# State-space chunks placed between the convolution branch's matmul units of a two-block transformer kernel

## What is computed

```python
h = x @ w_in
sc_b, sc_c, sc_h, z, xbc, dt_raw = _split(h, [...])
y_a = sc_b * causal_dwconv(sc_c * sc_h, sc_conv_w)               # convolution branch, 3 taps
xs, bm, cm = _split(silu(causal_dwconv(xbc, ssm_conv_w, ssm_conv_b)), [...])
# state-space branch: 4 chunks of 128 tokens, 16 heads of 64, 2 groups, state 128
seg = exp(where(causal, a_cs[t] - a_cs[s], -inf))                # a_cs: running sum of dt * a
cb = einsum('bctgn,bcsgn->bcgts', cc, bc)
y_diag = einsum('bcgts,bcgrts,bcsgrp->bctgrp', cb, seg, xdt)
y_off = cc @ (state carried from the chunks before), scaled by exp(a_cs)
y = y_diag + y_off + d_skip * xs
y_b = gated_rmsnorm(y, z, norm_g)
mixer = concatenate([y_a, y_b]) @ w_out
```

## Time and profile before

| | |
|---|---|
| time, median of 3 runs | 2885.03 us |
| time of the profiled execution | 2883.41 us |
| span of its trace | 2881.5 us |
| PE busy in the span | 2821.4 us |
| DVE, ACT, POOL busy | 1341.6, 1078.1, 1147.8 us |
| DMA, mean over the span | 104 GB/s |

### The profile page before, as it was taken

How to read it: one execution, slowest core, us unless ns; L and a number is a source line. 1 busy time by engine, 2 the same in 40 slices (tenths; PEclk the granted TensorE clock), 3 DMA queues, 4 the chain that set the end, 5 groups by cost and what they waited for, 6 DMA issues and landing times.

```text
span 2881.5 us, 37694 instructions
## 1 busy us (share of the span) xinstructions
PE 2821.4 (98%) x13730; PEld 2306.2 (80%) x13730; DVE 1341.6 (47%) x1532; ACT 1078.1 (37%) x1524; POOL 1147.8 (40%) x472
## 2 busy tenths in 40 slices
PE   9998799999999999999989999999999999999999
PEld 8787588888878778888877778888888888888887
DVE  4332837885345457886347753113332742321232
ACT  4322244333344344334344653234342323432332
POOL 4442044444434203444424223444434434444443
PEclk9999799999999999999999999999999999999999
DMA  5332025763233104873323013332343223333332
GB/s 158 93 94 67 0 88 182 242 217 102 81 99 92 52 8 131 259 239 108 102 66 100 2 52 88 95 103 94 102 125 102 83 79 102 95 88 95 105 99 73
DMA packets 319809, 299.90 MB, mean 104 GB/s; under 512 B 16268, under 2 KB 251224, under 8 KB 319576
## 3 DMA queue, kind: packets, MB, share of 16 engines
q1 hardware_dynamic: 304680, 236.70, 27.9%
q10 hardware_dynamic: 15024, 61.75, 6.3%
HBM read 296.30 MB, written 2.11 MB: 104 GB/s over the span
## 4 chain that ended last, share of the span: by engine, by line
PE 45%; issue 37%; POOL 16%; DVE 1%; ACT 0%; POOLq 0%; DVEq 0%; ACTq 0%
POOL wlo L548 16%; PE ps L1992 7%; PE ps L1993 7%; PE ps L1994 7%; PE ps L1850 6%; PE ps L1851 6%; PE ps L1852 6%; PE ps L2222 1%; PE ps L2165 1%; PE ps L2191 1%; PE ps L2297 1%; PE ps L2016 0%; PE ps L2018 0%; PE ps L2017 0%; PE ps L1855 0%
## 5 line engine op out<-in xcount | busy, mean ns | idle before, releaser
L548 POOL TENSOR_TENSOR wlo<-raw,whi 128x1024 fp32r<-128x1024 f32 x444 | 1122.6, 2531 | 1695.3 <-ACT whi L606 1695.0
L1850 PE MATMUL ps<-xhi,whi 128*128 128x512 f32 x1824 | 714.7, 392 | 1.8 <-DVE pb L1233 1.5
L1852 PE MATMUL ps<-xhi,wlo 128*128 128x512 f32 x1824 | 710.1, 389 | 0.0
L1851 PE MATMUL ps<-xlo,whi 128*128 128x512 f32 x1824 | 709.9, 389 | 0.0
L606 ACT ACTIVATE whi<-raw 128x1024 fp32r<-128x1024 f32 x444 | 466.2, 1051 | 343.4 <-PE ps L1994 171.9
L1992 PE MATMUL ps<-whi,ahi 128*128 128x512 f32 x1184 | 463.0, 391 | 8.9 <-issue 7.8
L1994 PE MATMUL ps<-whi,alo 128*128 128x512 f32 x1184 | 462.3, 390 | 0.0
L1993 PE MATMUL ps<-wlo,ahi 128*128 128x512 f32 x1184 | 462.2, 390 | 0.0
L1850 PEld LDWEIGHTS ps<-xhi,whi 128*128 128x128 f32 x1824 | 342.4, 188 | 74.3 <-DVE pb L1233 1.9
L1852 PEld LDWEIGHTS ps<-xhi,wlo 128*128 128x128 f32 x1824 | 342.3, 188 | 71.7
L1851 PEld LDWEIGHTS ps<-xlo,whi 128*128 128x128 f32 x1824 | 342.5, 188 | 69.3
(11 more groups left out here) (277 smaller groups left out, 2940.7 us busy)
## 6 DMA issues: line engine op xcount, KB each, us to landing
adaraw<-in_ada_w ACTq DMA_DIRECT2D x64, 768.0 KB, 6.1
raw<-in_ffn_w_up SPq DMA_DIRECT2D x88, 512.0 KB, 4.0
raw<-in_mlp_w_in SPq DMA_DIRECT2D x64, 512.0 KB, 4.1
raw<-in_mlp_w_out SPq DMA_DIRECT2D x64, 512.0 KB, 3.6
raw<-in_gmlp_w_in SPq DMA_DIRECT2D x48, 512.0 KB, 3.8
raw<-in_sc_ssm_w_in SPq DMA_DIRECT2D x44, 512.0 KB, 3.8
raw<-in_ffn_w_down SPq DMA_DIRECT2D x44, 512.0 KB, 3.6
raw<-in_fox_w_in SPq DMA_DIRECT2D x24, 512.0 KB, 3.8
```

The source lines that it names most:

```text
L548: pool.tensor_tensor(wlo[:, j], raw[:, j], whi[:, j].bitcast(F32), ALU.subtract).then_inc(w_lo, 1)
L1850: pe.matmul(out, lh, rh, start=start, stop=False)
L1851: pe.matmul(out, lh, rl, start=False, stop=False)
L1852: return pe.matmul(out, ll, rh, start=False, stop=stop)
```

## The change

The units of `z` come right after those of `xbc`, and their silu is taken then. The 16 units of `scp` and the 8 of `scb` are written out one by one (`pe_mix`, `act_mix`, `dve_mix`, v = 0 to 23), and behind fixed ones of them each engine does a piece of the state-space work on banks 0 to 3, which the units don't use: the transposes behind units 0 to 2 (`TOK_AT`), the running sums behind 3 (`CUMS_AT`), and for each chunk the decay matrix (`R_AT`), the C B product and the carried part (`CB_AT`), an addition (`OFF_IN_AT`), and the head matmuls with the state (`Y_AT`).

The decay matrix is made in another way. PE transposes the running sum of each head, broadcast over 128 columns, 16 transposes a chunk; ScalarE takes relu(a_s - a_t) per head straight out of PSUM (16 instructions of 128 by 128, with `scale=-1` and the sum as bias), and then exp(-x). `gbuf`, the matmuls with ones, DVE's subtraction and its clamp are gone. y is built up in place in `xs_tok`, and `xdt`, `xdd` have one buffer each. The 32 transposes in front of the second part of `out0` are split in two groups of 16, behind its second and its third unit.

```diff
+UNITS = [("xbc", 12), ("z", 8), ("scp", 16), ("scb", 8), ("out0", 16), ("up0", 44), ("dn0", 22),
          ("fqk", 16), ("fv", 8), ("fo", 8), ("up1", 44), ("dn1", 22), ("qkv", 12), ("o", 8),
          ("mu0", 32), ("md0", 32), ("gv", 24), ("gu", 24), ("go", 24), ("mu1", 32), ("md1", 32)]
...
+MIX = 24
+TOK_AT, CUMS_AT = (0, 1, 2), 3
+R_AT = (4, 9, 14, 19)
+CB_AT = (5, 10, 15, 20)
+OFF_IN_AT = (6, 11, 16, 21)
+Y_AT = (7, 12, 17, 21)
...
+    mbuf = arena("mbuf", [P, 16, P], 32)
+    ssd_sq = arena("ssd_sq", [P, 2, HALF], 32)
+    xdt = arena("xdt", [P, D], 40)
+    xdd = arena("xdd", [P, D], 44)
+    y_off = arena("y_off", [P, D], 76)
+    prev = arena("prev", [P, D], 80)
+    cbm = arena("cbm", [P, 2, P], 84)
...
         sp_f(sp, "xbc", w_in0, XBC_COL)
+        sp_t(sp, "z", w_in0, 4, [ZCOL, ZCOL + HALF])
         sp_pairs(sp, "scp", w_in0, SC_C, SC_H, 16)
         sp_f(sp, "scb", w_in0, SC_B)
-        sp_t(sp, "z", w_in0, 4, [ZCOL, ZCOL + HALF])
...
+        for v in range(MIX):
+            act_whi(act, S + AHEAD, v, v % 4)
+            if v < 16 and v % 2:
+                i, b = v // 4, v % 4 // 2
+                act.wait_ge(unit_done, S + v + 1)
+                if i:
+                    act.wait_ge(sc_step, 8 * i + 4 * b - 6)
+                act.activation(hb[:, b], ps[:, bank_f(v)], ACT.Copy).then_inc(sc_h, 1)
+            act_ssd_at(act, v)
+
...
+            act.wait_ge(dts, 15)
+            act.activation(sm[:, 12], sm[:, 15], ACT.Exp).then_inc(dta, 1)
+            act.activation(sm[:, 13], sm[:, 11], ACT.Exp).then_inc(dta, 1)
+            act.activation(sm[:, 14], ps[:, 0, 64:128].rearrange("p (c h) -> p c h", c=NT), ACT.Exp).then_inc(dta, 1)
...
+        if v in R_AT:
+            c = R_AT.index(v)
+            if c:
+                act.wait_ge(ssd_mm, c)
+                act.wait_ge(gt_sq, 2 * c)
+            for h in range(HEADS):
+                if h % 8 == 0:
+                    act.wait_ge(ssd_r, 2 * c + h // 8 + 1)
+                act.activation(mbuf[:, h], ps[:, h // 4, (h % 4) * P:(h % 4 + 1) * P], ACT.Relu, scale=-1.0,
+                               bias=sm[:, 11, c, h:h + 1]).then_inc(ssd_d, 1)
             for g in range(2):
-                act.wait_ge(ssd_d, 4 * c + 2 * g + 2)
-                act.activation(mbuf[:, 8 * g:8 * g + 8], mbuf[:, 8 * g:8 * g + 8], ACT.Exp).then_inc(ssd_e, 1)
-            if c:
-                act_gate_squares(act, c - 1)
-
-    def act_gate_squares(act, t):
-        act.wait_ge(gt_u, t + 1)
-        for g in range(2):
-            if t or g:
-                act.wait_ge(gt_sq, 2 * t + g)
-            act.activation(ssd_sq[:], y_tok[:, t, g * HALF:(g + 1) * HALF], ACT.Square,
-                           accum_out=sumsq[:, t, g:g + 1]).then_inc(gt_sq, 1)
+                m = mbuf[:, 8 * g:8 * g + 8]
+                act.wait_ge(ssd_d, 16 * c + 8 * g + 8)
+                act.activation(m, m, ACT.Exp, scale=-1.0).then_inc(ssd_e, 1)
+        if v in Y_AT:
+            c = Y_AT.index(v)
+            act.wait_ge(gt_u, c + 1)
+            for g in range(2):
+                act.activation(ssd_sq[:, g], xs_tok[:, c, g * HALF:(g + 1) * HALF], ACT.Square,
+                               accum_out=sumsq[:, c, g:g + 1]).then_inc(gt_sq, 1)
...
-        act.wait_ge(ssd_mm, 4)
+        act.wait_ge(scb_done, 8)
         split(0, 0, 0, 0)
         split(1, 0, 0, 1)
-        act_gate_squares(act, NT - 1)
         act.wait_ge(gt_sq, 8)
         act.activation(mv[:], sumsq[:], ACT.Sqrt, scale=1.0 / HALF, bias=eps_ln[:, 0:1]).then_inc(gt_std, 1)
...
+    def dve_scp(dve, v):
+
+        i, b = v // 4, v % 4 // 2
+        k, s = 2 * i + b, 8 * i + 4 * b + 1
+        y = ya_yb[:, k]
+        dve.wait_ge(sc_h, k + 1)
...
+        for v in range(MIX):
+            if v < 16 and v % 2:
+                dve_scp(dve, v)
+            dve_ssd_at(dve, v)
+            if v >= 16:
+                e = v - 16
+                if e == 0:
+                    dve.wait_ge(sc_step, 33)
+                dve.wait_ge(unit_done, S + v + 1)
+                dve.tensor_tensor(ya_yb[:, e], ps[:, bank_f(e)], ya_yb[:, e], ALU.mult).then_inc(scb_done, 1)
...
+        if v in R_AT:
...
+            dve.tensor_tensor(heads(xdt[:]), x, bc_h(sm[:, 9, c]), ALU.mult).then_inc(ssd_x, 1)
...
-            dve.wait_ge(ssd_x, 2 * c + 1)
...
+            dve.tensor_tensor(heads(xdd[:]), heads(xdt[:]), bc_h(sm[:, 12, c]), ALU.mult).then_inc(ssd_x, 1)
+            dve.tensor_tensor(x, x, bc_h(small[:, 2]), ALU.mult).then_inc(ssd_y, 1)
+        if v in CB_AT:
...
+            dve.wait_ge(ssd_cb, c + 1)
+            dve.tensor_tensor(cbm[:], ps[:, 0, 0:256].rearrange("p (g t) -> p g t", g=2),
+                              tri.unsqueeze(1).to_broadcast([P, 2, P]), ALU.mult).then_inc(ssd_cbm, 1)
+            if c:
+                dve.wait_ge(ssd_off, c)
+                dve.tensor_tensor(heads(y_off[:]), ps[:, 2:4].rearrange("p b (h d) -> p (b h) d", d=HD),
+                                  bc_h(sm[:, 13, c]), ALU.mult).then_inc(ssd_y, 1)
...
-            for g in range(2):
                 dve.wait_ge(ssd_e, 2 * c + g + 1)
...
+                dve.tensor_tensor(m, m, cbm[:, g].unsqueeze(1).to_broadcast([P, 8, P]), ALU.mult).then_inc(ssd_m, 1)
+        if v in OFF_IN_AT[1:]:
+            c = OFF_IN_AT.index(v)
+            dve.wait_ge(ssd_y, 4 * c)
+            dve.tensor_tensor(xs_tok[:, c], xs_tok[:, c], y_off[:], ALU.add).then_inc(ssd_y, 1)
...
+                dve.wait_ge(ssd_prev, 2 * c - 1)
+                dve.tensor_tensor(heads(prev[:]), heads(prev[:]), bc_h(sm[:, 14, c]), ALU.mult).then_inc(ssd_prev, 1)
...
             dve.wait_ge(ssd_mm, c + 1)
             if c < NT - 1:
...
-            ystep(dve.tensor_tensor(y, ps[:, 4:6].rearrange("p b n -> p (b n)"), y, ALU.add))
+            dve.wait_ge(ssd_y, 4 * c + 1)
+            dve.tensor_tensor(y, ps[:, 0:2].rearrange("p b n -> p (b n)"), y, ALU.add).then_inc(ssd_y, 1)
...
             dve.tensor_tensor(y, y, zs[:, c], ALU.mult).then_inc(gt_u, 1)
...
                 unit(1, 0, 0, False)
+                if mid:
+                    mid(pe)
                 unit(2, 0, 0, False)
                 head(pe)
...
+        S = U0["z"]
+        for h in range(2):
+            if h == 0:
+                pe.wait_ge(xbc_conv, 36)
+            else:
+                pe.wait_ge(dts, 1)
...
+        for v in range(MIX):
+            if v >= 20:
+                pe.wait_ge(scb_done, v - 19)
+            elif v >= 4:
+                pe.wait_ge(sc_step, 8 * (v // 4) + 4 * (v % 4 // 2) - 6)
+            pe.wait_ge(w_lo, S + v + 1)
...
+            ins.then_inc(unit_done, 1)
+            pe_ssd_at(pe, v)
...
+        if v in TOK_AT:
+            if v == 0:
+                pe.wait_ge(xbc_silu, 12)
+                pe.wait_ge(z_done, 8)
+            for g in range(4 * v, 4 * v + 4):
...
+        if v in R_AT:
+            c = R_AT.index(v)
+            if c == 0:
+                pe.wait_ge(dts, 15)
+                pe.wait_ge(dta, 6)
+            else:
+                pe.wait_ge(ssd_y, 4 * c - 2)
+                pe.wait_ge(ssd_prev, 2 * c - 1)
+            for h in range(HEADS):
+                ins = pe.transpose(ps[:, h // 4, (h % 4) * P:(h % 4 + 1) * P],
+                                   sm[:, 11, c, h:h + 1].to_broadcast([P, P]), ident)
+                if h % 8 == 7:
+                    ins.then_inc(ssd_r, 1)
...
+            pe.wait_ge(ssd_d, 16 * c + 8)
...
+            ins.then_inc(ssd_cb, 1)
             if c:
-                pe.wait_ge(ssd_y, ny[c - 1])
+                pe.wait_ge(ssd_d, 16 * c + 16)
...
+        if v in Y_AT:
+            c = Y_AT.index(v)
...
             for h in range(HEADS):
                 if h % 8 == 0:
                     pe.wait_ge(ssd_m, 2 * c + h // 8 + 1)
...
+        pe_z(pe)
+        pe_mix(pe)
+        pe_t_jit(pe, "out0", q=1, free=lambda h: ((ssd_y, 14),) if h == 0 else ((gt_ev, 8),),
+                 mid=lambda pe: pe_gate_tp(pe, 0), head=lambda pe: pe_gate_tp(pe, 4))
```

More of the change, by code:

```diff
@@ L678, in act_soft_log @@
         act.activation(sm[:, 7], sm[:, 4], ACT.Ln).then_inc(s_act, 1)
[L680 to L689, removed]
     def act_plain(act, name):
@@ new lines, in act_z, with act_mix @@
+        for e in range(8):
+            act_whi(act, S + AHEAD, e, e % 4)
+            if e == 0:
+                act_narrow(act, 0)
+            if e == 2:
+                act_soft_exp(act, dts, dta)
+            if e == 3:
+                act_soft_log(act, dts, dta)
+                act.wait_ge(small_in, 16 * 5)
+                act.activation(sm[:, 8, 0], small[:, 1], ACT.Exp).then_inc(dta, 1)
+            if e == 4:
+                silu(0)
+        silu(1)
+    def act_mix(act):
+        S = U0["scp"]
+        for v in range(MIX):
[7 more added lines that the diff above has]
+            act_ssd_at(act, v)
@@ L1243, in dve_scb @@
-    def dve_scb(dve):
-        S = U0["scb"]
-        dve.wait_ge(sc_step, 33)
-        def unit(e, j):
```

(53 more changed lines are left out.)

229 lines of the change are left out of this document (66 added, 163 removed).

## The result

| | before | changed |
|---|---|---|
| time, median of 4 runs each | 2884.83 us (2884.33 to 2886.07) | 2832.61 us (2831.32 to 2833.72) |
| profiled execution: time, span | 2883.41, 2881.5 us | 2831.32, 2829.4 us |
| mean granted clock over the span | 0.989 | 0.996 |

The ratio is 0.9818, with a 95% interval of 0.9806 to 0.9829: 52.2 us faster (50.1 forecast, 2834 us predicted, range 2826 to 2852).

What follows compares the result with a forecast made beforehand. PE was taken as the bound, busy 2821.4 of 2881.5 us, with 90.04 us in a state-space stage without weight tiles. 95.2 us saved less 37.3 of pieces and 7.8 of waits gave 50 us: 2834 us, range 2826 to 2852.

Steps and rivals of the forecast that it cites:

- What goes away: Separate state-space stage 90.04 us, `scb` wait 1.5, slow `out0` start 2.55, unit after the 32 transposes 1.13: 95.2 us in all.
- PE's pieces: State-space work put back on PE between the units, at full clock: 37.3 us in all.
- The head matmuls: Per chunk, in the pieces on PE: 3.2 us, four times, 12.8 us (9.2 to 14.1).
- the two rows weighed: For a chunk's head matmuls: half of 7.06 us, 3.5; or 32 records at 7 in 0.5 us, 2.3.
- The repeated column: Stationary operand of the decay matrix's 64 transposes: plain price of 0.115 us each, 7.4 us; at most twice, 14.7.
- Seams: At the 16 insertions, changing from fp32 transposes back to unit matmuls: 0.1 to 0.3 us each, 2 us in all.
- Wait at chunk 0's decay matrix: Behind unit 4, PE waits for exps of running sums: chain 6.8 us against 5.9 of PE work, 0.9 us.
- Start of `out0`: First split waits for unit 23's last product, `scb_done` 8: 3.2 us of wait, then 1.7 us of slower matmuls.
- Covers: ScalarE and DVE work at the insertions stays hidden under units; thinnest cover 1.8 us, at chunk 3.
- Rival 1: At the insertions DVE or ScalarE comes late, four mask-product waits return, 16.8 us: 2851 us; chance 0.12.
- rivals 2, 3 and 4: 2: clock falls in head matmuls, 2862 us, 0.08; 3: at every insertion, 2912 us, 0.03; 4: pieces dearer, 2854 us, 0.05.

Runs made afterwards that it cites:

- the fourfold transposes: The changed kernel with the 16 decay-matrix transposes of each chunk done four times over: 2853.69 us, ratio to before 0.9893.
- the kernel with the early head matmuls: The changed kernel with the head matmuls of chunks 0 to 2 one unit earlier (behind units 6, 11, 16): 2845.23 us, ratio to before 0.9865.
- The kernel with early splits: The changed kernel with the first two `out0` splits behind unit 22, waiting for `scb_done` 2 and 4: 2827.83 us; again 2828.35 against 2832.39 us for the change.
- the repeated pieces: Two versions of the changed kernel: each chunk's 16 transposes done four times, 2853.69 us; each chunk's head matmuls done three times, 2861.13 us.
- the kernel with DVE's clamp: The changed kernel with subtraction and clamp back on DVE and ScalarE's 64 relus gone, transposes kept: 2832.12 us, ratio to before 0.9817.

## Why the prediction was right

The mechanism was right, and the sum (50.1 us) was 2.1 us short of the 52.2 measured. Two slips of arithmetic do not touch it: 2833.3 and 1.6 us are 2834.9 us and not 2834, and the upper ends of the terms' own spread add up to 16 us, 2850 us and not 2848. By its steps:

- **What goes away**: the stage of 90.04 us is gone, as is the wait at the start of `scb` and most of that behind the transposes in `out0` (0.39 us is left for 0.84; none was forecast).
- **PE's pieces**: 37.3 us forecast; with their seams they take about 38.7 by the distances between starts. The head matmuls were taken too low (3.51 us for 3.2, 1.2 us in all); of the two rows weighed, half of the 7.06 us was the right one. The repeated column was taken rightly at the plain price, which the fourfold transposes confirm.
- **Seams**: 2 us were charged and none are needed. The long first matmul behind a piece (0.47 us) overlaps the piece's last record and is already in the distances above: from the first transpose at 163.50 to the C B products at 170.72 us are 7.22 us, a unit and 1.78.
- **Wait at chunk 0's decay matrix**: 0.9 us was charged, none came. The chain was taken from a pair whose taps ended 5.75 us after `hb` began. Here it was shorter:

```profile
158.40 0.69 DVE L1252 TENSOR_TENSOR pb<-ps,hb 128x512 f32<-128x512 f32 x1 [5.68 <-ACT hb L722]
159.13 0.49 DVE L1254 TENSOR_SCALAR ya_yb<-pb,tab 128x512 f32<-128x512 f32 x1
159.65 1.54 DVE L1258 SCALAR_TENSOR_TENSOR ya_yb<-pb,tab,ya_yb 128x511 f32<-128x511 f32 x2
161.10 0.22 DVE L1292 COPY sm<-ps 128x64 f32<-128x64 f32 x1
```

  The taps end 3.4 us after `hb` began at 157.77, with no `wlo` running from 156.09 to 163.15 us. The 5.75 us had such an overlap in it: in the trace of before a `wlo` runs from 100.92 to 103.57 us, and the tap that starts at 101.51 beside it takes 2.60 us, the next one 0.75. ScalarE's table load did run in the time it waited for DVE, as assumed:

```profile
158.39 1.28 ACT L736 ACT_TABLE_LOAD   x1
161.61 0.26 ACT L736 ACTIVATE sm<-sm 128x64 f32<-128x64 f32 x1 [1.94 <-DVE sm L1294]
...
164.58 4.24 ACT L747 ACTIVATE mbuf<-ps,sm 128x128 f32<-128x128 f32 x16 [1.50 <-PE ps L2127]
```

- **Start of `out0`**: 3.2 us of wait and 1.7 us of slow clock forecast. The wait is 3.18 us; the window from 304 us, 5 us at 0.66, is 1.7 us lost. That the slow part came out as forecast is luck: in the second profile of the change the same wait of 3.18 us is followed by a mean of 0.54 from 303.85 to 310.50 us, 3.1 us lost, and in the kernel with the early head matmuls (316 to 326 us) the clock does not fall behind it. The kernel with early splits takes both away and gains 4.0 us.
- **Covers**: 4.5 us for the relus (4.24 measured), enough at every place. But they were thinner than I counted. At chunk 3, called the thinnest with 1.8 us, the two mask products took 4.55 us for 2.36:

```profile
280.91 1.23 DVE L1317 TENSOR_TENSOR y_off<-ps,sm 128x1024 f32<-128x1024 f32 x1 [1.29 <-PE ps L2141]
282.05 4.55 DVE L1323 TENSOR_TENSOR mbuf<-mbuf,cbm 128x1024 f32<-128x1024 f32 x2
```

  They end at 286.60 us, 0.4 us after the head matmuls began at 286.20. PE was not held up only because the second product is wanted 8 heads later, half of 3.51 us, so some 1.4 us were left. The thinnest cover was at chunk 0, which the prediction had not called thin: its first mask product, drawn out to 3.12 us, ended at 181.50 us, and PE came to it at 182.06 us, 0.56 us later. This is the step in which I was lucky: the durations of DVE were taken from a stage in which GpSimd was idle (2.37 us busy of 72) and used in one where it runs a third of the time. The 12.6 us of the early head matmuls are what the same error costs one unit further.

Rival 1 had the right place and failed by that margin of 0.56 us; rivals 2, 3 and 4 fell with the repeated pieces. The errors that I can name are +1.2 for the head matmuls against -2 for seams and -0.9 for the wait, 1.7 us of the 2.1 in which the sum fell short.

## What to carry to other kernels

Put serial small work under dense matmuls before making it cheaper: the place was worth 62.6 us, and the rest of the change without the place lost 10. When counting a cover, take the durations of DVE beside the work that GpSimd will be doing there, not from a stage in which it is idle, and allow for a wait of 2 to 3 us of PE costing twice its length and more, since slow matmuls can follow it. And let a consumer wait for the part that it reads (here `scb_done` 2 and 4 for 8), which gave 4.0 us.

## What the runs showed of the hardware

- DVE operations with two operands in SBUF and GpSimd's `wlo` exclude each other: two taps take 3.54 us for 1.53, a product of 1.2 us becomes 3.4, and `wlo` itself, 2.40 us alone, takes 3.05 at 163.15 us where DVE was first. The scaling ahead of the taps (L1254), which reads one wide operand, is drawn out too: 1.52 us for 0.49 (at 172.91 us).
- The clock held at 1.00 through 64 transposes (7.15 us) and through 10.2 us of 64-column matmuls, each behind dense units. Every fall seen before PE's last matmul, in the traces looked at, begins in or soon after a wait of PE. The length of the wait does not tell alone. None followed the 0.39 us before 331.66 us. The 1.94 us before 1529.82 us was followed by one in the change (0.79 from 1528 to 1536 us), while in the kernel with DVE's clamp the window from 1528 to 1536 us, with the same wait in it, is at 1.00. And 2.58 us for `vtok`, before 921.45 us, had none behind it in the change (1.00 from 921 to 935 us), but one in the kernel before (0.79 from 972 to 980 us).
